# Three products of a split matrix multiplication, block by block or pass by pass, in the feed-forward units of a two-layer decoder trunk

## What is computed

```
def finish(x, m, w_o, g_post_mix, g_pre_ffn, g_post_ffn, w_gate, w_up, w_down):
    x = x + rmsnorm(m @ w_o, g_post_mix)
    h = rmsnorm(x, g_pre_ffn)
    f = (jax.nn.silu(h @ w_gate) * (h @ w_up)) @ w_down
    return x + rmsnorm(f, g_post_ffn)
```

## Time and profile before

| | us |
|---|---|
| median of 3 runs | 3132.66 |
| lowest and highest of them | 3129.66, 3135.19 |
| the profiled execution, its time | 3102.04 |
| its span, first to last instruction | 3100.3 |

### The profile page before, as it was taken

The page is one execution under the profiler, slowest core; times in us unless marked ns, Lnnn a source line. Parts: engine busy times, 40 slices in busy tenths (PEclk is TensorE's granted clock), DMA queues, the critical chain, the costliest instruction groups (busy, mean ns, idle before and its releaser), DMA issues. The chain is left out here.

```text
span 3100.3 us, 48849 instructions
## 1 busy us (share of the span) xinstructions
PE 3011.1 (97%) x19766; PEld 2644.6 (85%) x19766; DVE 1434.6 (46%) x3278; ACT 1053.9 (34%) x2094; POOL 734.4 (24%) x526
## 2 busy tenths in 40 slices
PE   8999999989999999999999999899999999999998
PEld 6777766669999999999977777665799999999997
DVE  5579675557611111122565887565574111111125
ACT  4376535554311111011333665355542111110112
POOL 3002041324312122243300201313352122121131
PEclk9999999999999999999999999999999999999999
DMA  5120235651211111121321111456411111111131
GB/s 181 37 64 28 70 150 172 226 204 49 71 44 48 48 47 43 48 66 59 113 79 45 47 35 50 181 184 228 169 58 60 48 48 42 48 48 48 41 118 56
DMA packets 254071, 263.54 MB, mean 85 GB/s; under 512 B 24993, under 2 KB 224570, under 8 KB 253850
## 3 DMA queue, kind: packets, MB, share of 16 engines
q1 hardware_dynamic: 233370, 189.11, 19.5%
q0 software_dynamic: 20480, 71.32, 6.6%
HBM read 229.73 MB, written 30.65 MB: 84 GB/s over the span
## 5 line engine op out<-in xcount | busy, mean ns | idle before, releaser
L2199 PE MATMUL ps<-act_lo,w_hi 128*128 128x352 f32 x2112 | 684.2, 324 | 5.0 <-DVE act_lo L2651 3.1
L2199 PE MATMUL ps<-act_hi,w_hi 128*128 128x352 f32 x2112 | 677.9, 321 | 0.0
L2199 PE MATMUL ps<-act_hi,w_lo 128*128 128x352 f32 x2112 | 677.2, 321 | 0.0
L2573 POOL TENSOR_TENSOR w_lo<-w_raw,w_hi 128x1024 fp32r<-128x1024 f32 x132 | 322.0, 2441 | 1022.9 <-ACT w_hi L2413 1022.8
L709 PE MATMUL ps<-w_in_slots,hT 128*128 128x256 f32 (+1 forms) x2048 | 448.5, 375 | 3.4 <-PEq L192 3.4
L709 PEld LDWEIGHTS ps<-w_in_slots,hT 128*128 128x128 f32 x2048 | 374.7, 193 | 58.6 <-issue 12.4
L2199 PEld LDWEIGHTS ps<-act_lo,w_hi 128*128 128x128 f32 x2112 | 396.7, 188 | 10.2 <-issue 5.2
L2664 DVE TENSOR_TENSOR a_raw<-ps,silu 128x352 f32<-128x352 f32 x120 | 63.0, 525 | 728.7 <-PE ps L2199 728.7
L2199 PEld LDWEIGHTS ps<-act_hi,w_hi 128*128 128x128 f32 x2112 | 397.4, 188 | 0.2
L2199 PEld LDWEIGHTS ps<-act_hi,w_lo 128*128 128x128 f32 x2112 | 396.5, 188 | 0.0
L2199 PE MATMUL ps<-a_lo,w_hi 128*128 128x352 f32 x1056 | 344.1, 326 | 0.0
(11 more groups left out here) (368 smaller groups left out, 4255.2 us busy)
## 6 DMA issues: line engine op xcount, KB each, us to landing
w_raw<-in_w_gate SPq DMA_DIRECT2D x44, 512.0 KB, 3.8
w_raw<-in_w_up SPq DMA_DIRECT2D x44, 512.0 KB, 3.8
w_raw<-in_w_down SPq DMA_DIRECT2D x44, 512.0 KB, 3.8
w_in_slots<-in_w_in SPq DMA_DIRECT2D x18, 1024.0 KB, 5.3
xpark<-xT SPq DMA_DIRECT2D x9, 1408.0 KB, 5.7
xT<-xpark SPq DMA_DIRECT2D x6, 1408.0 KB, 15.5
hT<-xpark SPq DMA_DIRECT2D x6, 1408.0 KB, 12.8
wo_raw<-in_w_o SPq DMA_DIRECT2D x16, 512.0 KB, 5.2
```

What stands on the lines that cost most here:

```text
L2199: ins = pe.matmul(bank(b), w, x, start=first and i == 0, stop=end and i == 2)
L2573: pool.tensor_tensor(w_lo[slot(j)][:, 0:K, :], w_raw[slot(j)][:, 0:K, :], w_hi[slot(j)][:, 0:K, :].bitcast(F32), ALU.subtract).then_inc(w_ ...
```

## The change

```diff
+            def factors(what, k, th):
+                return (a_hi[k][:, of(th)], a_lo[k][:, of(th)]) if what == "down" else (act_hi[:, k, of(th)], act_lo[:, k, of(th)])
+
             for n, (j, th) in enumerate(seq):
...
-                for k in range(K):
-                    if j == 0:
-                        pe.wait_ge(h_lo, KC * th + k + 1)
-                    if what == "down" and i == 0:
-                        pe.wait_ge(a_lo_done, up_nth[chunk(p_, k), th])
-                    x_hi, x_lo = (a_hi[k][:, of(th)], a_lo[k][:, of(th)]) if what == "down" else (act_hi[:, k, of(th)], act_lo[:, k, of(th)])
-                    ins = terms(unit_bank(n), w_hi[slot(j)][:, k, :], w_lo[slot(j)][:, k, :], x_hi, x_lo, k == 0, k == K - 1)
+                if j < NPRE or what == "down" and i == 0:
+                    for k in range(K):
+                        if j == 0:
+                            pe.wait_ge(h_lo, KC * th + k + 1)
+                        if what == "down":
+                            pe.wait_ge(a_lo_done, up_nth[chunk(p_, k), th])
+                        ins = terms(unit_bank(n), w_hi[slot(j)][:, k, :], w_lo[slot(j)][:, k, :], *factors(what, k, th), k == 0, k == K - 1)
+                else:
+                    for k in range(K):
+                        pe.matmul(bank(unit_bank(n)), w_hi[slot(j)][:, k, :], factors(what, k, th)[1], start=k == 0, stop=False)
+                    for k in range(K):
+                        pe.matmul(bank(unit_bank(n)), w_hi[slot(j)][:, k, :], factors(what, k, th)[0], start=False, stop=False)
+                    for k in range(K):
+                        ins = pe.matmul(bank(unit_bank(n)), w_lo[slot(j)][:, k, :], factors(what, k, th)[0], start=False, stop=k == K - 1)
                 ins.then_inc(mm, 1)
```

## The result

| | before | changed |
|---|---|---|
| median, us (6 runs each) | 3133.62 | 3146.73 |
| lowest, highest | 3129.66, 3135.6 | 3140.81, 3149.44 |
| ratio, 95% interval | | 1.0045 (1.0035 to 1.0055) |
| profiled execution, span | 3100.3 | 3147.7 |

The changed kernel is slower by 13.1 us between the medians, 0.42%, clear of the 0.2% that a measurement can't tell from nothing. The page of the changed kernel answers to the earlier trace rows: the same counts, the same shares.

The account below looks back on a forecast made before the run. TensorE's unbroken matmul stream was taken as the bound, 159.27 ns per matmul in the changed stretch. Gate and up +5.2 and down -1.6 gave +3.6 us on 3132.66, so 3136.3 us; whole range 3124 to 3150.

Parts of the forecast that it names:

- The term of gate and up: Gate and up matmuls: pitch from 159.0 to 159.9 ns, times 5,760, +5.2 us; ends -4.0 and +16.7 us.
- seven stretches: Seven parts of the earlier trace without a wait, in gate and up, down and `mix`, with pitches 158.3 to 161.9 ns.
- The bounds, 158.3 and 161.9: Lowest and highest pitch in ns of any stretch read, taken as limits for the new order.
- The term of down: Down matmuls: pitch from 160.0 to 159.2 ns, times 2,016, -1.6 us; ends -3.4 and +3.8 us.
- the slower rhythm: Rival: gate and up settle at 161.2 ns, down at 160.0; +12.7 us, 3145 us; chance 0.30.
- the 161.2 stretch of `mix`: Second third of `mix`, d = 3 to 6, 95 steps, read at 161.2 ns; cited for the slower rival.
- Repeated reading: Rival: no `w_hi` block read twice in a row saves 3 ns per triple, -7.8 us, 3125; chance 0.13 with another lucky rhythm.
- the competition goes away: Rival: row reading and weight loads stop competing, pitch falls to 147 ns, -96 us, 3037 us; chance 0.02.
- a competition between rows and weight loads: Supposed: reading 352 columns competes with the next weights' load beside it, costing 11 to 15 ns per matmul.
- a difference under 0.2%: The forecast's own case: pitch within 0.8 ns of now, total within 6.3 us; chance 0.53.
- the sixth stretch of the prediction: Second third of `mix`, d = 3 to 6, 95 steps from 721.74 to 737.05, read at 161.2 ns.
- the fifth: Second third of `mix`, d = 0 and 1, 47 steps from 709.66 to 717.13, read at 158.9 ns.

Follow-up runs that it names:

- e9: Kernel before, gate and up blocks replaced by 40 openings, then strictly alternating rows: per layer 8 stretches at 158.33 ns, 32 at 161.67.
- e7: Kernel before, gate and up blocks from block 4 replaced by 20 patterns of rows, weights and columns; with 352 columns 158.33 to 161.67 ns.
- e2: Changed kernel with k as 0, 2, 4, 6, 1, 3, 5, 7 in each pass and down in the old order: ratio 1.0006 against before.
- e8: Kernel before with all large buffers 128 bytes lower: one run, 3129.52 us against 3128.4 for one of the kernel before.
- e11: Changed kernel with gate and up alternating unbroken from third to third, down in the old order: 3117.66 us, ratio 1.0052 against before.
- e12: As e11, with the third and fourth matmul exchanged in 6 units: 3099.37 us, ratio 0.9989 against the kernel before.

## Why the prediction came out as it did

**Where the time is: right.** Instructions, waits, signals and loads were costed at nothing, and their rows did not move. The windows grew to 650.18 us (638 to 655 had been given), and 16.0 us of them are the change.

**The term of gate and up: mis-sized.** I took the mean of seven stretches, 159.9 ns, for an order that none of them had, and got +5.2 us. It measured 161.67, 2.67 ns above before: 2.67 x 5,760 = +15.4 us. The step that failed is the mean. An alternating stream has two steady rhythms, 158.33 and 161.67 (e9), and the mean of the list was none of the values that it could take. The bounds, 158.3 and 161.9, were the right use of these rows: both rhythms lie within them. In part that was luck, since 161.67 stands in none of the seven and the upper bound came from 16 steps of the last down, which has another order.

**The term of down: wrong in sign, and small.** -1.6 us was expected, +0.5 came (0.27 ns x 2,016). Two thirds of the columns went to 159.7, the middle one to 161.4. That tiles two apart behave like one row read again was an assumption. For `act_hi` rows it holds (e7: k = 0 and 2 in turn, 160.0 and 161.1, as k = 0 alone); why it doesn't give 159.2 here, and why the middle third is slower, is not settled.

**The rivals.** What happened is the slower rhythm, which I had at 0.30: the changed kernel went where the 161.2 stretch of `mix` had pointed. That the stream had changed its rhythm there by a wait does not fit the trace, which has two other matmuls in its place and no idle time (last section). My point against it, that before the mean stayed at 159.27 in both layers, told of another order of rows. Repeated reading, which would have made the old order dear, is out: in e2 no block is read twice in a row and its gate and up are at 159.18 ns, not below the 158.99 of before, and a single weight block all the time runs at 158.33 ns with k = 1, just as changing blocks do (e7). That the competition goes away is out as well: every pitch from 256 columns up carries at least 11 ns. My sentence on a competition between rows and weight loads holds so far: the pitch depends on where the two lie towards each other (e7, e8). What in the chip the 13.3 ns are is not shown.

**The total.** 3136 us against 3146.73: inside the range of 3124 to 3150, outside the forecast's own 3126 to 3139. The case that I held likeliest, a difference under 0.2% at 0.53, did not come; slower had 0.32. So the range held by its width and not by the sum. The term of gate and up makes up 10.2 us of the 12.4 by which the windows' 16.0 passed my 3.6; down makes up the other 2.1.

## What to carry to other kernels

Where one engine is busy without a gap, a reordering can change its pitch: multiply 1 ns by the number of instructions before calling an order free. Read the pitch in a window around the edited code from the starts, for the two profiled spans here differed by 30 us in other stages. Rows of a moving operand that are a whole multiple of 256 bytes long had one pitch here (256, 320 and 512 columns of 4 bytes; alternating starts were tried with 320); with 352 columns order and entry decide over 3.3 ns. And where a quantity has shown distinct steady values, price each of them, not their mean.

## What the runs showed of the hardware that had not been expected

- A stream of dense 128x352 float32r matmuls keeps a rhythm over hundreds of matmuls (48 units, 1,152 matmuls, in e11 and e12) and the same sequence can run at 158.33 or 161.67 ns. The order of five matmuls at its start decides (e9); in e12 the exchange of two was enough.
- Where every matmul has its own weight load, the pitch is 13.3 ns above the columns / 2.4, for 256, 320 and 512 columns alike, and with 192 or 128 columns it is 111.7 ns.
- Only the relative place of activations and weights within 256 bytes mattered for the blocks: a common shift by 96 or 128 bytes changed their windows by 0.02 us. It is not without any effect: four units of `mix` in the second third (d = 3 to 6, 95 steps) ran at 161.1 ns in both layers before and after the change (the sixth stretch of the prediction), and at 158.9 in both layers of e8, where nothing but addresses differs:

```profile
736.19:751.28 15.09, 15.09 (x97) 15.09 (x96) 12.77 (x16) 6.98 (x16) 11.50 (x11) 1.00 0.08 28
2281.70:2296.80 15.10, 15.10 (x98) 15.10 (x97) 12.77 (x16) 6.99 (x16) 11.50 (x11) 1.00 0.08 27
```

- The same code can also change its rhythm between the layers of one run: four units of `mix` in the last third (d = 2 to 5, 95 steps) ran at 160.0 ns in layer 0 of the kernel before and at 158.9 in layer 1:

```profile
751.04:766.24 15.20, 15.20 (x97) 15.20 (x96) 14.96 (x18) 6.41 (x16) 9.45 (x9) 1.00 0.00 0
2283.40:2298.50 15.10, 15.10 (x98) 15.10 (x96) 15.00 (x18) 6.32 (x16) 9.31 (x9) 1.00 0.00 1
```

- What sets a rhythm anew need not be a wait. One unit ahead of each of these stretches two matmuls of line 2203 stand in the stream, and no idle time; in layer 0 of the kernel before, between the fifth and the sixth stretch of the prediction, which put their difference down to a wait:

```profile
717.13 0.32 PE L2199 MATMUL ps<-act_hi,wo_lo 128*128 128x352 f32 x1
717.29 0.75 PE L2203 MATMUL ps<-mix_acc,ones 128*128 128x352 f32 x2
717.61 0.59 PE L2199 MATMUL ps<-act_lo,wo_hi 128*128 128x352 f32 x1
```

That these two are what changes the rhythm is likely, but no run tested it.
